# Taking the scores of a batch's new keys two steps earlier in a merged attention

## The chip, the core and the metric

The program runs on one core of a Trainium2 chip. The metric is the device time of one execution in microseconds (us). Before the change the median of three runs is 2041.23 us, from 2040.16 to 2042.34. All times of rows below come from one profiled execution of 2040.47 us, whose span from its first to its last instruction is 2038.8 us.

## What is computed

One inference step of a hybrid decoder layer, for a prompt of 1024 tokens and for 8 decoding batches of 8 new tokens each, every one with 4096 cached keys in 32 pages of 128. The part that matters here is differential attention: 4 heads, each with two query/key sub-heads of 64 dimensions and a value of 128. A decoding batch attends to its pages and, under a causal mask, to its own new keys, in one softmax:

```python
def diff_attend_sample(q, k, v, lam, k_past, v_past):
    s_past = jnp.einsum('bqhcd,bkhcd->bhcqk', q, k_past).astype(F32) * scale
    s_new = jnp.einsum('bqhcd,bkhcd->bhcqk', q, k).astype(F32) * scale
    s_new = jnp.where(jnp.tril(jnp.ones((T, T), dtype=bool)), s_new, -jnp.inf)
    a = jax.nn.softmax(jnp.concatenate([s_past, s_new], axis=-1), axis=-1)
    w = (a[:, :, 0] - lam * a[:, :, 1]).astype(v.dtype)
    return (jnp.einsum('bhqk,bkhv->bqhv', w[..., :P], v_past)
            + jnp.einsum('bhqk,bkhv->bqhv', w[..., P:], v))
```

The maximum of a softmax row thus spans the scores of all pages and those of the new keys. Projections, gated linear attention, output projection, feed-forward and a per-layer embedding stand before and after this part.

## The kernel before

The kernel is written in stages. The stage of interest, the function `attention`, merges two jobs in one order written out by hand: attention over the prompt (units of one head and 128 queries, 32 in all) and attention of the decoding batches over their pages. It lies between about 519 and 945 us of the span.

A group is 4 pages, 512 keys. A batch has NG = 8 groups, so there are NKV = 64. Every engine walks through the same steps t = 0 to 73, and in each it does what belongs to the step: the keys of group t are transposed (`turn_keys`, heads 0 to 3), scored against the batch's queries one step later (`score(t - 1)`), and their maximum and copy are taken by VectorE another step later (`max_scores(t - 2)`, `copy_scores(t - 2)`). The weights of group v = t - 9 (LAG = NG + 1) are made by ScalarE (`exps`), transposed (`turn_p`) and multiplied with the values (`values`): only when all 8 groups of a batch and its new keys are scored is its maximum known. Steps are counted by batch below: step 8b+9 is the end of batch b, where the last maximum is taken and the first weights are made.

Every second step has in between the prompt's work: `prompt_scores` on TensorE, which wait for ScalarE's last prompt exponentials; `prompt_maxima` on VectorE (mask, maximum, negated maximum), `prompt_exps` on ScalarE, `prompt_turn` (weights transposed) and `prompt_out` on TensorE.

What sets the order:
- The engines run their own lists in order; semaphores join them. An instruction that waits holds all that stands behind it on its engine.
- A ring of three PSUM banks (class `Ring`) takes every transposed key head, the transposed weights, the merge of a batch's output and the scores of the new keys, in the order in which TensorE fills them. A slot may be filled again when its last owner, three places before, has been emptied by ScalarE (key heads 0 to 2, merge) or by VectorE (the rest). `emptied(key)` is that wait on TensorE.
- The new keys of batch b: `score_new(b)` stands on TensorE at step 8(b+1), behind `score`. VectorE's `take_new(b)` stands in the next step between `max_scores` and `copy_scores`: it adds the mask into `dec_s` (which frees the ring slot, L1609), takes the maximum (L1611), the maximum over the nine columns of `mx` (L1613) and the negated scaled maximum (L1615), on which ScalarE's `exps` of the batch's first group wait.
- At a batch's end ScalarE makes the first weights (L1331), the weights of the new keys (L1336), and only then copies key head 2 (L1320, `take_keys(t, 2)`). The transpose of the new keys' weights (`turn_new_p`, L1454) has the ring slot that this copy empties.
- GpSimd asks for a group's value pages when the values of four groups before are done; SP for key pages when all heads of four groups before are transposed.

Names of rows: `dec_k`, `dec_v` pages; `dec_kt` transposed keys; `dec_s` scores; `dec_p`, `dec_pn` weights of a group and of the new keys; `att_p`, `att_wt` the prompt's weights and their transposes; `att_small` small columns such as maxima; `dec_osc` a batch's scaled output.

Of the kernel before, what the change touches and what calls it, by code (L numbers as in the profile page):

```python
# [15 lines left out]
ALU = mybir.AluOpType  # L16
ACT = mybir.ActivationFunctionType
AX = mybir.AxisListType
# [5 lines left out]
DB, DS = 8, 8  # L24
# [44 lines left out]
class Memory:  # L69


    def __init__(self, nc):
        self.nc, self.n = nc, 0
# [1021 lines left out]
NG = NPG // 4  # L1095
NKV = DB * NG
LAG = NG + 1
STEPS = NKV + LAG + 1
UNITS = [(h, i) for h in range(H) for i in (0, 7, 1, 6, 2, 5, 3, 4)]
NU = len(UNITS)  # L1100
# [7 lines left out]
def pieces_of(n):  # L1108
    return 1 if blocks_of(n) <= 4 else 2
# [6 lines left out]
class Ring:  # L1116
# [4 lines left out]
    def __init__(self):  # L1121
        self.index, self.emptied, self.owners = {}, {}, []
        count = {"act": 0, "dve": 0}

        def use(key, owner):
            self.index[key] = len(self.owners)
            count[owner] += 1
            self.emptied[key] = count[owner]
            self.owners.append((owner, count[owner]))

        for t in range(STEPS):
            if t < NKV:
                for h in range(H):
                    use(("keys", t, h), "act" if h < 3 else "dve")
            b, last = divmod(t - LAG - NG, NG)
            if last == 0 and 0 <= b < DB:
                use(("merge", b), "act")
            v = t - LAG
            if 0 <= v < NKV:
                if v % NG == 0:  # L1140
                    use(("new_p", v // NG), "dve")
                use(("p", v), "dve")
            b, last = divmod(t - NG, NG)
            if last == 0 and 0 <= b < DB:
                use(("new_s", b), "dve")

# [32 lines left out]
def attention(nc, io, m, ps, scr, sems):  # L1179
# [14 lines left out]
    d = {n: sems("p4_" + n) for n in names.split()}  # L1194
# [11 lines left out]
    W_BANK, S_BANK, O_BANK = bank(5), bank(6), bank(7)  # L1206
# [4 lines left out]
    mx, esum, ssum, cs, negm = (m.sc[:, 24:33], m.sc[:, 34:52].rearrange("p (u g) -> p u g", u=2), m.sc[:, 52:54],  # L1211
                                m.sc[:, 54:56], m.sc[:, 56:58])
# [18 lines left out]
    with nc.Block() as block:  # L1231
# [49 lines left out]
        def _(act):  # L1281
# [17 lines left out]
            def copy_weights(n, q):  # L1299

                i, u = UNITS[n][1], n % 2
                a, b = 4 * q * P, min(4 * q + 4, i + 1) * P
                act.wait_ge(s["turned"], pieces_before(n) + q + 1)
                if n >= 1:
                    act.wait_ge(s["o_done"], n)
                act.activation(m.wt[:, a:b], W_BANK[:, 0:b - a], ACT.Copy).then_inc(s["wt_copied"], 1)
# [33 lines left out]
            def copy_os(b):  # L1340
                act.wait_ge(d["ring_filled"], ring.filled(("merge", b)))
                act.activation(m.os[:, b, :], ring_bank(("merge", b))[0:32, 0:DV], ACT.Copy).then_inc(d["ring_act"], 1)

            for t in range(STEPS):
                v = t - LAG
                n, c = divmod(t, 2)
# [15 lines left out]
                if c == 1 and 0 <= n - 1 < NU and pieces_of(n - 1) == 2:  # L1362
                    copy_weights(n - 1, 1)
                if t >= LAG + NG and (t - LAG - NG) % NG == 0:
                    copy_os((t - LAG - NG) // NG)
                if t == HALVES:
# [8 lines left out]
        def _(pe):  # L1375
# [37 lines left out]
            def emptied(key):  # L1413
                before = ring.before(key)
                if before is not None:
                    pe.wait_ge(d["ring_act" if before[0] == "act" else "ring_dve"], before[1])
# [24 lines left out]
            def score_new(b):  # L1441
                if b == 0:
                    pe.wait_ge(d["new_in"], 32)
                key = ("new_s", b)
                emptied(key)
                for h in range(H):
                    ins = pe.matmul(ring_bank(key)[32 * h:32 * h + 32, 0:NS], m.qb[:, b % 2, h, :], m.kts[:, h, :],
                                    start=True, stop=True, tile_position=(0, 32 * h))
                ins.then_inc(d["ring_filled"], 1)
# [34 lines left out]
            def merge(b):  # L1484
                pe.wait_ge(d["final"], 4 * b + 4)
                emptied(("merge", b))
                pe.matmul(ring_bank(("merge", b))[0:32, 0:DV], const(m, "merge"), m.osc[:, :], start=True, stop=True
                          ).then_inc(d["ring_filled"], 1)

            pe.wait_ge(d["zero_done"], 4)  # L1490
            for t in range(STEPS):
                v = t - LAG
                n, c = divmod(t, 2)
                if t < NKV:
                    turn_keys(t, 0)
                    turn_keys(t, 1)
                if c == 0 and 0 <= n - 2 < NU:
                    prompt_out(n - 2)
                if c == 1 and 0 <= n - 1 < NU:
                    prompt_turn(n - 1, 0)  # L1500
                if t < NKV:
                    turn_keys(t, 2)
                    turn_keys(t, 3)
                if t >= LAG + NG and (t - LAG - NG) % NG == 0:
                    merge((t - LAG - NG) // NG)
                if 0 <= v < NKV:
                    if v % NG == 0:
                        turn_new_p(v // NG)
                    turn_p(v)
                if c == 1 and 0 <= n - 1 < NU and pieces_of(n - 1) == 2:  # L1510
                    prompt_turn(n - 1, 1)
                prompt_scores(t)
                if 1 <= t <= NKV:
                    score(t - 1)
                if t and t % NG == 0 and t // NG <= DB:
                    score_new(t // NG - 1)
                if 0 <= v < NKV:
                    values(v)

        @block.vector  # L1520
        def _(dve):
# [68 lines left out]
            def max_scores(k):  # L1590
                b, g = divmod(k, NG)
                dve.wait_ge(d["s_full"], k + 1)
                dve.tensor_reduce(mx[:, g:g + 1], S_BANK, AX.X, ALU.max)

            def copy_scores(k):
                b, g = divmod(k, NG)
                if b:
                    dve.wait_ge(d["exp_done"], k - NG + 1)
                dve.tensor_copy(m.ss[:, 512 * g:512 * g + 512], S_BANK).then_inc(d["s_taken"], 1)

            def take_new(b):

                key = ("new_s", b)
                dve.wait_ge(d["ring_filled"], ring.filled(key))
                dst = m.ss[:, PAST:PAST + NS]
                if b:
                    dve.wait_ge(d["expn_done"], b)
                a = CONST_COLS["past"][0] + 56 - b * DS
                dve.tensor_tensor(dst, ring_bank(key)[:, 0:NS], m.consts[:, a:a + NS], ALU.add).then_inc(d["ring_dve"], 1)  # L1609
                dve.wait_ge(d["ring_dve"], ring.emptied[key])  # L1610
                dve.tensor_reduce(mx[:, NG:NG + 1], dst, AX.X, ALU.max).then_inc(d["mx"], 1)  # L1611
                dve.wait_ge(d["mx"], b * 2 + 1)
                dve.tensor_reduce(ssum[:, 1:2], mx, AX.X, ALU.max).then_inc(d["mx"], 1)  # L1613
                dve.wait_ge(d["mx"], b * 2 + 2)
                dve.tensor_scalar(negm[:, b % 2:b % 2 + 1], ssum[:, 1:2], -SC, None, ALU.mult).then_inc(d["negm"], 1)  # L1615

            def take_new_p(b):
# [31 lines left out]
            queries(0)  # L1649
            for t in range(STEPS):  # L1650
                v = t - LAG
                n, c = divmod(t, 2)
                if t >= LAG + NG and (t - LAG - NG) % NG == 0:
                    finalize((t - LAG - NG) // NG)
                if 0 <= t - 2 < NKV:
                    max_scores(t - 2)
                if 0 < t - 1 <= NKV and (t - 1) % NG == 0:
                    take_new((t - 1) // NG - 1)
                if 0 <= t - 2 < NKV:
                    copy_scores(t - 2)  # L1660
                if t < NKV:
                    take_keys(t, 3)
                if 0 <= v < NKV:
                    if v % NG == 0:
                        take_new_p(v // NG)
                    take_p(v)
                if c == 0 and 0 <= n - 1 < NU:
                    prompt_combine(n - 1)
                prompt_maxima(t)
                if t % NG == 4 and t // NG + 1 < DB:  # L1670
                    queries(t // NG + 1)
                if t >= LAG + NG - 1 and (t - LAG - NG + 1) % NG == 0:
                    final_scale((t - LAG - NG + 1) // NG)
                if HALVES < t <= HALVES + H:
                    norm_prompt(t - HALVES - 1)
# [890 lines left out]
```

## Time and profile before

| what | value |
|---|---|
| median of three runs | 2041.23 us (2040.16 to 2042.34) |
| profiled execution, its own time | 2040.47 us |
| its span | 2038.8 us |
| TensorE busy, share of the span | 1863.9 us, 91% |
| TensorE weight loads | 1718.4 us, 84% |
| VectorE | 971.9 us, 48% |
| ScalarE | 608.9 us, 30% |
| GpSimd | 397.2 us, 19% |
| HBM traffic over the span | 114 GB/s |

Shares of the whole span are averages over stages with different limits. For a change within the merged attention only rows of that stage tell: who waits there, and for whom. A row of a timeline has the start in us, the time it took, engine, line, operation, what is written and read, a count, and in brackets how long the engine had been idle before it and what released it. PE is TensorE, PEld its weight loads, DVE is VectorE, ACT ScalarE, POOL GpSimd. Where TensorE works almost without a break, ends of matmuls overlap the next start, since they are pipelined.

### The profile page before, as it was taken

How to read it: one execution, taken by the hardware profiler on the slowest of the kernel's cores; microseconds unless marked ns; L12 is line 12 of the kernel's file. 1: busy time of each engine (PE TensorE's matmuls, PEld its weight loads, DVE VectorE, ACT ScalarE, POOL GpSimd, SP SyncE). 2: the span in 40 equal slices, each digit the busy share in tenths (PEclk: the TensorE clock that was granted, in tenths of full speed). 3: DMA queues.
4: the chain of work that ended last, by engine and by line, in shares of the span. 5: the costliest groups of instructions: out<-in, count | busy, mean ns of one | idle time of the engine just before them, and what ended most of it. 6: DMA issues, size and time to landing. Idle time of an engine off the chain costs nothing. (4 is left out here: it accounts for less than half of the span.)

```text
span 2038.8 us, 35290 instructions
## 1 busy us (share of the span) xinstructions
PE 1863.9 (91%) x13412; PEld 1718.4 (84%) x13412; DVE 971.9 (48%) x1356; ACT 608.9 (30%) x1086; POOL 397.2 (19%) x393
## 2 busy tenths in 40 slices
PE   4999999575899999996999999999999999998898
PEld 4999999463566767664898999999999999998798
DVE  4223730486677777775325334344334333436443
ACT  4113321442465655563322211111111111113320
POOL 1112420232123333332112011101101110104110
PEclk9999999696899999998999999999999999999899
DMA  4332640204799999987111111111111111110221
GB/s 141 97 85 76 156 114 21 65 3 145 247 329 348 360 337 366 356 257 228 32 42 52 47 47 32 52 43 49 45 42 42 42 53 42 32 54 20 85 64 44
DMA packets 201583, 239.02 MB, mean 117 GB/s; under 512 B 15425, under 2 KB 142354, under 8 KB 201426
## 3 DMA queue, kind: packets, MB, share of 16 engines
q1 hardware_dynamic: 180946, 169.75, 27.0%
q0 software_dynamic: 20480, 67.13, 9.7%
q8 instruction: 105, 1.72, 0.4%
q14 instruction: 52, 0.43, 0.1%
HBM read 215.44 MB, written 16.91 MB: 114 GB/s over the span
## 5 line engine op out<-in xcount | busy, mean ns | idle before, releaser
L150 PE MATMUL psum<-h_hi,w_hi 128*128 128x364 f32 x1248 | 278.7, 332 | 2.8 <-issue 2.8
L150 PE MATMUL psum<-h_lo,w_hi 128*128 128x364 f32 x1248 | 276.3, 330 | 0.0
L150 PE MATMUL psum<-h_hi,w_lo 128*128 128x364 f32 x1248 | 275.2, 328 | 0.0
L2078 ACT ACTIVATE w_hi<-w_raw 128x1024 fp32r<-128x1024 f32 x66 | 68.8, 1059 | 586.3 <-PE psum L150 565.5
L150 PEld LDWEIGHTS psum<-h_hi,w_hi 128*128 128x128 f32 x1248 | 215.4, 189 | 4.9 <-issue 4.2
L150 PEld LDWEIGHTS psum<-h_lo,w_hi 128*128 128x128 f32 x1248 | 217.1, 189 | 0.0
L150 PEld LDWEIGHTS psum<-h_hi,w_lo 128*128 128x128 f32 x1248 | 216.7, 188 | 0.0
L2054 POOL TENSOR_TENSOR w_raw<-w_raw,gains 128x1024 f32<-128x1024 f32 x42 | 80.5, 1916 | 652.2 <-DMA w_raw<-in_w_ffn_gate 353.0
L1163 POOL DMA_DIRECT2D dec_v<-in_cache_v x256 | 137.5, 537 | 316.6 <-issue 316.6
L150 PE MATMUL psum<-x_hi,w_hi 128*128 128x364 f32 x792 | 188.5, 347 | 9.7 <-DVE x_lo L1911 5.8
L150 PE MATMUL psum<-x_hi,w_lo 128*128 128x364 f32 x792 | 176.5, 331 | 0.0
L150 PE MATMUL psum<-x_lo,w_hi 128*128 128x364 f32 x792 | 176.3, 331 | 0.0
L2194 DVE TENSOR_TENSOR h<-h,psum 128x1092 f32<-128x1092 f32 x88 | 113.5, 1289 | 108.0 <-PE psum L150 108.0
L150 PEld LDWEIGHTS psum<-x_hi,w_hi 128*128 128x128 f32 x792 | 137.3, 191 | 16.5 <-DVE x_lo L1911 6.3
L1425 PE MATMUL psum<-consts,dec_k 128*128 128x128 f32 x1024 | 139.7, 281 | 12.2 <-DVE dec_s L1609 6.1
L1320 ACT ACTIVATE dec_kt<-psum 128x512 f32<-128x512 f32 x192 | 108.4, 599 | 139.8 <-PE psum L1425 139.8
L1425 PEld LDWEIGHTS psum<-consts,dec_k 128*128 128x128 f32 x1024 | 115.2, 143 | 31.6 <-issue 17.0
L150 PEld LDWEIGHTS psum<-x_lo,w_hi 128*128 128x128 f32 x792 | 139.4, 190 | 0.0
L150 PEld LDWEIGHTS psum<-x_hi,w_lo 128*128 128x128 f32 x792 | 138.9, 190 | 0.0
L2173 DVE TENSOR_TENSOR t_up<-psum,rstd_and_sum 128x1092 f32<-128x1092 f32 x22 | 28.5, 1296 | 205.9 <-PE psum L150 205.9
L150 PE MATMUL psum<-hidden_hi,w_hi 128*128 128x364 f32 x528 | 116.9, 330 | 2.5 <-DVE w_lo L2164 2.5
L150 PE MATMUL psum<-hidden_lo,w_hi 128*128 128x364 f32 x528 | 117.4, 331 | 0.0
(262 smaller groups left out, 2793.4 us busy)
## 6 DMA issues: line engine op xcount, KB each, us to landing
dec_k<-in_cache_k SPq DMA_DIRECT2D x256, 256.0 KB, 5.1
dec_v<-in_cache_v POOLq DMA_DIRECT2D x256, 256.0 KB, 5.2
w_raw<-in_w_in SPq DMA_DIRECT2D x25, 512.0 KB, 3.9
w_raw<-in_w_ffn_gate SPq DMA_DIRECT2D x22, 512.0 KB, 3.9
w_raw<-in_w_ffn_up SPq DMA_DIRECT2D x22, 512.0 KB, 3.8
w_raw<-in_w_ffn_down SPq DMA_DIRECT2D x22, 512.0 KB, 3.6
feat_swap<-feat_n SPq DMA_DIRECT2D x32, 136.5 KB, 2.4
x_in<-in_x_prompt SPq DMA_DIRECT2D x4, 1024.0 KB, 8.2
```

The costliest lines, as they stand in the source:

```text
L150: ins = pe.matmul(out[:, c, 0:SPAN], w(k), x(k)[:, c * SPAN:c * SPAN + SPAN], start=n == 0 and w is whi and x is xhi, stop=n == len(ks) - ...
L1163: eng.dma_start(ring[:, slot, p:p + 1, :], cache[bass.ds(page, 1)].rearrange("o t f -> t o f")).then_inc(sem, 16)
L1320: act.activation(m.kt[:, t % 2, h, :], ring_bank(("keys", t, h)), ACT.Copy).then_inc(d["ring_act"], 1)
L1425: ins = pe.transpose(ring_bank(key)[:, p * P:p * P + P], m.kr[:, t % KR, p, h * P:h * P + P], ident)
L2054: gp.tensor_tensor(m.raw[:, u], m.raw[:, u], gain(m, "ffn").unsqueeze(2).broadcast_to([P, KT, P]), ALU.mult).then_inc(s["w_scaled"], 1)
L2078: act.activation(m.whi[:, slot], m.raw[:, u], ACT.Copy).then_inc(s["w_hi"], 1)
L2173: dve.tensor_tensor(spans(dst), dense[bank][:, :, 0:SPAN], spans(m.rb[:, :]), ALU.mult).then_inc(s["evacuated"], 1)
L2194: dve.tensor_tensor(spans(m.h[:, n]), spans(m.h[:, n]), dense[n % 2][:, :, 0:SPAN], ALU.add).then_inc(s["evacuated"], 1)
```

## The change

`score_new` moves from step 8(b+1) to step 8b+6 of TensorE (NEW_AT = 6), and the entry of the ring with it. `take_new` keeps the mask add and the maximum of the new keys, and VectorE runs it in step 8b+7, behind the copy of that step's scores. The maximum over the nine columns and its scaling become `batch_max`, which stays at the batch's end. The last `max_scores` of a batch now raises the semaphore on which `batch_max` waits; before, the wait was on the new keys' maximum, which came behind it on the same engine.

```diff
+NEW_AT = NG - 2
...
-            b, last = divmod(t - NG, NG)
+            b, last = divmod(t - NEW_AT, NG)
             if last == 0 and 0 <= b < DB:
                 use(("new_s", b), "dve")
...
-                if t and t % NG == 0 and t // NG <= DB:
-                    score_new(t // NG - 1)
+                if t % NG == NEW_AT and t // NG < DB:
+                    score_new(t // NG)
                 if 0 <= v < NKV:
                     values(v)
...
-                dve.tensor_reduce(mx[:, g:g + 1], S_BANK, AX.X, ALU.max)
+                ins = dve.tensor_reduce(mx[:, g:g + 1], S_BANK, AX.X, ALU.max)
+                if g == NG - 1:
+                    ins.then_inc(d["mx"], 1)
...
                 dve.tensor_reduce(mx[:, NG:NG + 1], dst, AX.X, ALU.max).then_inc(d["mx"], 1)
-                dve.wait_ge(d["mx"], b * 2 + 1)
+
+            def batch_max(b):
+                dve.wait_ge(d["mx"], b * 3 + 2)
                 dve.tensor_reduce(ssum[:, 1:2], mx, AX.X, ALU.max).then_inc(d["mx"], 1)
-                dve.wait_ge(d["mx"], b * 2 + 2)
+                dve.wait_ge(d["mx"], b * 3 + 3)
...
                 if 0 < t - 1 <= NKV and (t - 1) % NG == 0:
-                    take_new((t - 1) // NG - 1)
+                    batch_max((t - 1) // NG - 1)
                 if 0 <= t - 2 < NKV:
                     copy_scores(t - 2)
+                if (t - 1) % NG == NEW_AT and (t - 1) // NG < DB:
+                    take_new((t - 1) // NG)
```

The orders of ScalarE, GpSimd and SP stay as they are. The changed file is a line longer at its head, so TensorE's lines count one more, VectorE's up to five.

TensorE, batch 1, from the prompt's scores of step 14 to the values of step 16, before (L1389 prompt scores, L1437 scores, L1447 scores of the new keys, L1479 values, L1425 key transposes, L1402 and L1460 transposes of the weights):

```order
L1389 MATMUL psum<-att_k_102,att_q 128x384 x2
L1437 MATMUL psum<-dec_kt,dec_qb 32x512 x4
L1479 MATMUL psum<-dec_v,dec_pt 32x128 x16
L1425 MATMUL psum<-consts,dec_k 128x128 x8
L1402 MATMUL psum<-consts,att_p 128x128 x4
L1425 MATMUL psum<-consts,dec_k 128x128 x8
...
L1389 MATMUL psum<-att_k_97,att_q 128x128 x2
L1437 MATMUL psum<-dec_kt,dec_qb 32x512 x4
L1447 MATMUL psum<-dec_new_k,dec_qb 32x64 x4
L1479 MATMUL psum<-dec_v,dec_pt 32x128 x16
```

The same stretch of TensorE in the changed kernel:

```order
L1390 MATMUL psum<-att_k_102,att_q 128x384 x2
L1438 MATMUL psum<-dec_kt,dec_qb 32x512 x4
L1448 MATMUL psum<-dec_new_k,dec_qb 32x64 x4
L1480 MATMUL psum<-dec_v,dec_pt 32x128 x16
L1426 MATMUL psum<-consts,dec_k 128x128 x8
L1403 MATMUL psum<-consts,att_p 128x128 x4
L1426 MATMUL psum<-consts,dec_k 128x128 x8
...
L1390 MATMUL psum<-att_k_97,att_q 128x128 x2
L1438 MATMUL psum<-dec_kt,dec_qb 32x512 x4
L1480 MATMUL psum<-dec_v,dec_pt 32x128 x16
```

The scores of the new keys stand in step 14, and the third key transpose behind them, in the ring's order, is head 2 of step 15.

VectorE, batch 1, steps 15 and 17 of the changed kernel; first step 15, from the maximum of the scores to the transposed weights (L1594 maximum, L1602 copy, L1612 mask add, L1614 maximum of the new keys, L1589 copy of key head 3, L1632 of the weights):

```order
L1594 TENSOR_REDUCE att_small<-psum 128x1
L1602 COPY dec_s<-psum 128x512
L1612 TENSOR_TENSOR dec_s<-psum,consts 128x64
L1614 TENSOR_REDUCE att_small<-dec_s 128x1
L1589 COPY dec_kt<-psum 128x512
L1632 COPY dec_pt<-psum 128x512
```

The third and fourth row are new in this step. At the batch's end, step 17, VectorE had before, from the scaled output to the copy of the scores:

```order
L1644 TENSOR_SCALAR dec_osc<-psum,att_small 128x128
L1593 TENSOR_REDUCE att_small<-psum 128x1
L1609 TENSOR_TENSOR dec_s<-psum,consts 128x64
L1611 TENSOR_REDUCE att_small<-dec_s 128x1
L1613 TENSOR_REDUCE att_small<-att_small 128x1
L1615 TENSOR_SCALAR att_small<-att_small 128x1
L1599 COPY dec_s<-psum 128x512
```

and has now:

```order
L1649 TENSOR_SCALAR dec_osc<-psum,att_small 128x128
L1594 TENSOR_REDUCE att_small<-psum 128x1
L1618 TENSOR_REDUCE att_small<-att_small 128x1
L1620 TENSOR_SCALAR att_small<-att_small 128x1
L1602 COPY dec_s<-psum 128x512
```

The mask add and the new keys' maximum are gone from this place.

## Rows read from the trace of the kernel before

**Rows 1.** Stretches: us, busy by engine (instructions), PEclk, DMA share, GB/s.

```profile
620.00:660.00 40.00, 38.14 (x481) 27.81 (x481) 28.99 (x57) 23.18 (x60) 13.41 (x25) 1.00 1.03 341
```

**Rows 2.** Waits for value pages and for the scores: engine, instruction, us, times.

```profile
  PE psum L1479: 8.7, 4
...
  DVE att_small L1615: 2.6, 7
...
  PE psum L1425: 6.1, 7
```

**Rows 3.** Timeline, all engines, end of batch 1 (step 17).

```profile
617.10 0.68 DVE L1593 TENSOR_REDUCE att_small<-psum 128x1 f32<-128x512 f32 x1
...
617.70 0.21 DVE L1609 TENSOR_TENSOR dec_s<-psum,consts 128x64 f32<-128x64 f32 x1
617.95 0.22 DVE L1611 TENSOR_REDUCE att_small<-dec_s 128x1 f32<-128x64 f32 x1
...
617.97 1.09 PE L1425 MATMUL psum<-consts,dec_k 128*128 128x128 f32 x8 [0.91 <-DVE dec_s L1609]
...
618.20 0.16 DVE L1613 TENSOR_REDUCE att_small<-att_small 128x1 f32<-128x9 f32 x1
618.40 0.15 DVE L1615 TENSOR_SCALAR att_small<-att_small 128x1 f32<-128x1 f32 x1
...
618.59 0.72 ACT L1331 ACTIVATE dec_p<-dec_s,att_small 128x512 f32<-128x512 f32 x1 [0.34 <-DVE att_small L1615]
...
618.99 0.41 PE L1487 MATMUL psum<-dec_osc,consts 128*32 128x128 f32 x2
...
620.36 0.30 PE L1454 MATMUL psum<-consts,dec_pn 128*128 128x128 f32 x1 [0.96 <-ACT dec_kt L1320]
```

**Rows 4.** Timeline, ScalarE, end of batch 2 (step 25).

```profile
668.81 0.72 ACT L1331 ACTIVATE dec_p<-dec_s,att_small 128x512 f32<-128x512 f32 x1 [0.21 <-DVE att_small L1615]
```

**Rows 5.** Timeline, TensorE, scores and values of steps 15 and 16.

```profile
608.03 1.07 PE L1437 MATMUL psum<-dec_kt,dec_qb 128*32 128x512 f32 x8
...
608.91 1.06 PE L1479 MATMUL psum<-dec_v,dec_pt 128*32 128x128 f32 x32
...
613.54 1.07 PE L1437 MATMUL psum<-dec_kt,dec_qb 128*32 128x512 f32 x8
...
614.54 1.06 PE L1479 MATMUL psum<-dec_v,dec_pt 128*32 128x128 f32 x32
```

**Rows 6.** Timeline, TensorE and VectorE, step 15 (8b+7 of batch 1).

```profile
605.35 1.04 PE L1425 MATMUL psum<-consts,dec_k 128*128 128x128 f32 x8
605.37 0.68 DVE L1599 COPY dec_s<-psum 128x512 f32<-128x512 f32 x1
...
606.22 0.60 PE L1460 MATMUL psum<-consts,dec_p 128*128 128x128 f32 x4
...
607.18 0.92 PE L1389 MATMUL psum<-att_k,att_q 64*128 64x384 f32 x4 [0.36 <-ACT att_p L1296]
...
608.14 0.43 DVE L1548 TENSOR_TENSOR psum<-psum,consts 128x256 f32<-128x256 f32 x1 [0.43 <-PE psum L1389]
```

**Rows 7.** Timeline, TensorE and VectorE, steps 7 (batch 0) and 23 (batch 2).

```profile
557.87 0.68 DVE L1599 COPY dec_s<-psum 128x512 f32<-128x512 f32 x1
...
559.17 1.13 PE L1389 MATMUL psum<-att_k,att_q 64*128 64x512 f32 x4 [1.01 <-ACT att_p L1296]
...
655.09 0.68 DVE L1599 COPY dec_s<-psum 128x512 f32<-128x512 f32 x1
...
657.11 1.13 PE L1389 MATMUL psum<-att_k,att_q 64*128 64x512 f32 x4 [0.58 <-ACT att_p L1296]
```

**Rows 8.** Timeline at the end of batch 7, then the stretch behind it.

```profile
917.38 0.48 PE L1454 MATMUL psum<-consts,dec_pn 128*128 128x128 f32 x1 [2.14 <-ACT dec_pn L1336]
...
922.28 0.54 POOL L1163 DMA_DIRECT2D dec_v<-in_cache_v  x1 [2.06 <-issue]
...
917.30:921.00 3.70, 3.62 (x47) 2.60 (x47) 0.98 (x2) 1.16 (x5) 1.61 (x3) 0.57 0.76 226
```

## The prediction

> **What bounds the kernel now.** I looked first at the stretch that the diff can touch, the merged attention between 519 and 945 us, by stretches. In a typical 40 us of it TensorE is busy for 38.14 us, VectorE for 28.99 and ScalarE for 23.18; the DMA engines are taken too, at 341 GB/s [rows 1]. Two bounds lie close together, so the waits have to decide. TensorE's waits for value pages are 8.7 us in 4 times [rows 2], all four after 930 us, where the last pages come in; for key pages it has none. Up to there the pattern of a batch repeats every 50 us (the same instruction starts at 618.59 and 668.81 [rows 3, 4]). So order and latency between engines bound this stage, not bytes, and time that TensorE gains or loses before its tail moves the end.
>
> Next I asked who waits for the new scores. TensorE's matmuls wait 6.1 us in 7 times for the mask add that frees their ring slot, and ScalarE 2.6 us in 7 times for the negated maximum [rows 2]. The first number looks like the prize. The timeline of one batch's end says otherwise.
>
> At the end of batch 1 (step 17) [rows 3], VectorE takes the last maximum at 617.10 us, then mask add, two reductions and the scaling at 618.40. The add ends at 617.91 and TensorE goes on at 617.97, after 0.91 us of waiting. But TensorE does not keep what it would win there: after two key transposes and the merge at 618.99 it stands again until 620.36, 0.96 us, for ScalarE, whose copy of key head 2 comes after both exponentials in its own order. ScalarE began the first at 618.59, having waited 0.34 us for the maximum. **Only those 0.34 us can be won.** Taking away the 0.91 us makes the second wait longer by as much. Batches 3 and 5 read the same; batches 2, 4 and 6 have 0.21 us in its place [rows 4], batch 0 nothing (7 waits for 8 batches), and batch 7 what is left of the 2.6: 2.6 - 3 x 0.34 - 3 x 0.21 = 0.95. **2.6 us is the ceiling.**
>
> **The change part by part.**
>
> *Batch end, VectorE.* Mask add and reduction leave, one wait comes in: the reduction over nine columns now waits for the last maximum to be written. That wait is not in the trace; the nearest one is that of the same reduction for the one before it: 617.95 plus 0.22, next start 618.20, so 0.03 us after the end [rows 3]. Its bounds are 0 and the 0.06 us that a release took to another engine; I take 0.03. The maximum lasts 0.68, so: 617.10 + 0.68 + 0.03 = 617.81 for the reduction, 0.20 later 618.01 for the scaling, where 618.40 was. **Gain 0.39 us** in the chain of the maximum. Behind the waiting reduction stand the copy of the last scores and the copy of key head 3, which come 0.39 earlier too.
>
> *Score matmuls, TensorE.* Four small matmuls move from step 8b+8 to 8b+6. With them a step's scores and values start 1.00 us apart (613.54 to 614.54), without them 0.88 (608.03 to 608.91) [rows 5]: 0.12 us that changes place. It issues no DMA, and the orders of ScalarE, GpSimd and SP are as before.
>
> *The new waiting place.* In a ring of three slots the third key transpose after the new scores gets their slot. That is now head 2 of step 8b+7 (b is the batch), and the mask add that frees it stands behind the copy of that step's scores. Batch 1, step 15 [rows 6]: copy at 605.37, add 0.60 later (the distance from maximum to add, 617.10 to 617.70), end after 0.21, TensorE 0.06 after that: 606.24. TensorE had begun these transposes at 605.35. So they come 0.89 us later, 0.77 of it waiting. Behind them stand head 3, the transposes of the weights, the prompt's scores, the batch's scores and the values. Weight transposes 0.87 later (605.35 to 606.22): 607.11; 0.60 for them: prompt scores at 607.71. They stood at 607.18, having waited 0.36 us for ScalarE, a chain that moves by the 0.12 only (607.30). That cover takes part of the wait, and **0.53 us** is left. The two added VectorE instructions there cost nothing more: the copy of head 3 behind them waits for TensorE anyway, and VectorE idled 0.43 us for the prompt scores at 608.14 [rows 6]. Those it waits for again, so from here all moves by 0.53: step 16's scores, its VectorE chain, and the last maximum of step 17.
>
> *Sum of a batch.* VectorE's maximum comes 0.53 - 0.39 = 0.14 us later. ScalarE was ready at 618.59 - 0.34 = 618.25 and is now at 618.25 + 0.53 - 0.12 = 618.66, before the 618.73 of the maximum. So the new weights, and with them TensorE, come **0.14 us later** in batches 1, 3 and 5, though the 0.91 us wait is gone. Batches 2, 4 and 6, step 23 for one [rows 7]: copy 655.09, add 655.69, TensorE 655.96, weights 656.83, prompt scores 657.43 where they stood at 657.11 (0.58 of cover): 0.32 later. Maximum 0.07 earlier; ScalarE, ready 0.21 earlier than it began, comes 0.20 later: it decides, 0.01 us earlier. Batch 0, step 7 [rows 7]: copy 557.87, TensorE 558.74; no weight transposes follow yet, so prompt scores 0.87 later at 559.61 for 559.17: 0.44, less 0.12, and ScalarE had not waited at the batch's end: 0.32 later. Batch 7, step 63, has the form of step 15: 0.14 later, and this reaches the end, since GpSimd starts the next page loads at 922.28 after 2.06 us of idling for a value step [rows 8].
>
> 0.32 + 3 x 0.14 - 3 x 0.01 + 0.14 = **0.85 us later**. The profiled execution would go from 2040.47 to 2041.3 us (span 2038.8 to 2039.7, with the 1.7 around it). It lies 0.76 below the median of the three runs; from the median 2041.23 I come to 2042.1.
>
> **Key and value pages.** SP's load of keys waits for head 3 of four steps before; that comes some 0.9 us later once in a batch. Four steps are 25 us of the batch's 50, and TensorE has waited for no key page, so I add nothing; if a page should be late after all, the price would be at most those 0.9 us less the cover, again within the range.
>
> **The rivals.**
> *The full gain.* If the add at step 8b+7 ran early enough not to hold TensorE, or its wait vanished in idle time, the ceiling stands: 2041.23 - 2.6 = 2038.6 us. For it: ScalarE's 2.6 us are real. Against: the copy and TensorE's transposes start within 0.02 us of each other (605.37, 605.35), and the slot comes after the copy.
> *The wait is not covered.* If the 0.89 us goes wholly into VectorE's chain, since the cover by ScalarE moves too, each batch loses 0.89 - 0.39 = 0.50: 8 x 0.50 = 4.0, and 2041.23 + 4.0 = 2045.2 us. The rows with 0.36 and 0.58 us of cover speak against it.
> *The clock, the slower side.* At batch 7's end TensorE waited 2.14 us in one piece, and the stretch after it, 917.3 to 921.0, shows a granted clock of 0.57, between the levels of 1.2 and 2.4 GHz [rows 8]; the new weights' transpose took 0.48 us there, 0.30 at batch 1 [rows 3, 8]. The change joins two waits into one: at batch 1 TensorE's key transposes would start at 617.97 - 0.91 + 0.41 = 617.47, the merge 1.02 later, through at 618.90, and TensorE would stand until 620.50: 1.6 us, where 0.91 and 0.96 stood apart. If that suffices for the drop, 3.7 us at 0.57 cost 0.43 x 3.7 = 1.6 us at each of seven ends: 11 us, and 2042.1 + 11 = 2053 us. It decides somewhere between 0.96 us, after which the clock stayed, and 2.14. Against it: TensorE's work around the batch's end is the same, only shifted.
> The Trainium skill (TensorE: Matmul & The Clock Gate, What's actually happening) says that the clock follows how busy the engine has lately been. By that rule the clock would stay, since the change hardly alters how much TensorE works and waits there, and the time would be the forecast's; the row after 2.14 us agrees in that the clock fell behind a pause.
> *It does not do what it says.* That the maximum is not nearer to the batch's end for ScalarE is my forecast already; its part in the time is priced above.
>
> **How the numbers follow.** Forecast (small shift, within some 1.5 us) 0.66; full gain 0.16; uncovered wait 0.12; clock 0.06. Some 0.2%, 4.1 us, is about what a measurement of this kernel can tell from no change. Forecast and full gain lie within it but for 0.02; the uncovered wait lies at its edge, half over; the clock is over. So faster 0.02, same 0.86, slower 0.12. The range goes from the full gain to the uncovered wait, 2038.6 to 2045.3 (with 0.1 for the median), and leaves out the clock and the outer ends.
>
> **What would show it.** In the changed profile TensorE should wait for the mask add 8 times some 0.8 us (1.5 in batch 0), now at step 8b+7; the wait of 0.91 us at the batch's end should be gone, and the one before the new weights' transpose should have grown from 0.96 to some 1.6 us. A batch should still take 50 us, within 0.2. A batch shorter by 0.3 us would show the full gain, by 0.5 longer the uncovered wait, and a granted clock under 1 at 620 us the clock.

## The result, and the profile after

The changed kernel takes 2045.91 us (median of seven runs, 2040.44 to 2050.30) where the kernel before takes 2040.44 in the runs beside it: ratio 1.0027, 95% interval 1.0014 to 1.0040. It is slower by some 5.5 us. The forecast was 2042.1, the range ended at 2045.3. Against the median of the runs beside it, the forecast shift of 0.85 us would have been 2041.3.

The profiled execution of the changed kernel is its fastest run, 2040.44 us with a span of 2038.8, the same as before. The loss is in its attention stage all the same: from the first key transpose to the first matmul of the output projection the stage takes 439.38 us (515.71 to 955.09), where it took 433.28 before (519.05 to 952.33). That is 6.1 us more. In this execution the part ahead of the stage, which is the same in both kernels, was 3.3 us shorter and the part behind it 2.8 us shorter.

First the step that I had costed. Timeline of step 15 of the changed kernel (start, us, engine, line, operation, count, in brackets the idle time before it), which answers to [rows 6]:

```profile
600.31 1.09 PE L1426 MATMUL psum<-consts,dec_k 128*128 128x128 f32 x8
...
601.59 0.68 DVE L1602 COPY dec_s<-psum 128x512 f32<-128x512 f32 x1
602.18 0.21 DVE L1612 TENSOR_TENSOR dec_s<-psum,consts 128x64 f32<-128x64 f32 x1
...
602.45 1.09 PE L1426 MATMUL psum<-consts,dec_k 128*128 128x128 f32 x8 [0.61 <-DVE dec_s L1612]
...
603.91 0.92 PE L1390 MATMUL psum<-att_k,att_q 64*128 64x384 f32 x4
```

The same step of the kernel before begins with

```profile
603.98 1.09 PE L1425 MATMUL psum<-consts,dec_k 128*128 128x128 f32 x8
```

The mask add comes 0.59 us after the copy, TensorE 0.06 after its end, and the prompt's scores no longer wait for ScalarE. From the first keys of the step (600.31) to these scores it is 3.60 us, where 603.98 to 607.18 were 3.20: 0.40 more, where the prediction has 0.53 less the 0.12 by which the step begins earlier. So this went as worked out, except that TensorE's wait is 0.61 us and not 0.77. Over the whole stage the waits for the scores' tile are (engine, instruction, us, times), answering to [rows 2]:

```profile
  DVE att_small L1620: 0.5, 1
...
  PE psum L1426: 4.5, 8
```

ScalarE's wait for the maximum is gone but for batch 7, and TensorE waits 8 times for the mask add at its new place: seven times 0.61 or 0.62 us, and in batch 0 only 0.20 (1.5 was expected), since it had already waited 1.07 us for a key page in the same step.

Then the batch's end. TensorE's merge and the transpose of the new keys' weights, with the scores behind them, at the ends of batches 1 and 2, answering to [rows 3]:

```profile
614.48 0.41 PE L1488 MATMUL psum<-dec_osc,consts 128*32 128x128 f32 x2
616.70 0.30 PE L1455 MATMUL psum<-consts,dec_pn 128*128 128x128 f32 x1 [1.81 <-ACT dec_kt L1321]
...
617.99 1.07 PE L1438 MATMUL psum<-dec_kt,dec_qb 128*32 128x512 f32 x8
...
666.93 0.30 PE L1455 MATMUL psum<-consts,dec_pn 128*128 128x128 f32 x1 [1.90 <-ACT dec_kt L1321]
...
669.20 1.93 PE L1438 MATMUL psum<-dec_kt,dec_qb 128*32 128x512 f32 x8
```

At the ends of batches 1 to 6 the two waits have become one of 1.81 to 1.91 us; at batch 0 it is 1.61, at batch 7 1.76. Behind batch 1 the eight score matmuls take 1.07 us as ever; behind batch 2 the same eight take 1.93. The view by stretches says why (start:end, length, busy us of PE, PEld, DVE, ACT, POOL, then the granted TensorE clock, DMA share, GB/s), for some 3.7 us behind the ends of batches 1 to 7 of the changed kernel:

```profile
616.70:620.40 3.70, 3.70 (x61) 2.55 (x62) 3.06 (x7) 1.13 (x4) 0.54 (x1) 1.00 1.02 322
...
666.90:670.60 3.70, 3.67 (x20) 1.77 (x24) 2.20 (x5) 1.34 (x4) 0.54 (x1) 0.62 1.06 354
...
718.50:722.30 3.80, 3.74 (x22) 1.90 (x26) 1.99 (x5) 1.13 (x4) 0.54 (x1) 0.56 1.03 343
...
770.20:774.00 3.80, 3.71 (x60) 2.46 (x60) 2.86 (x7) 1.34 (x4) 0.54 (x1) 1.00 1.05 384
...
820.30:824.00 3.70, 3.67 (x31) 1.95 (x35) 2.30 (x6) 1.13 (x4) 0.54 (x1) 0.65 1.05 345
...
872.00:876.00 4.00, 3.89 (x20) 2.08 (x24) 2.08 (x4) 1.34 (x4) 0.54 (x1) 0.57 1.05 346
...
920.31:924.11 3.80, 3.80 (x47) 2.74 (x47) 0.98 (x2) 1.13 (x4) 1.61 (x3) 0.55 0.82 247
```

and of the kernel before, behind the ends of batches 2, 3, 5 and 6:

```profile
670.58:674.38 3.80, 3.80 (x61) 2.50 (x62) 2.95 (x7) 1.34 (x4) 0.37 (x1) 1.00 1.05 360
720.49:724.29 3.80, 3.80 (x62) 2.65 (x63) 3.10 (x7) 1.13 (x4) 0.47 (x1) 1.00 1.05 343
...
820.69:824.49 3.80, 3.80 (x63) 2.71 (x64) 3.10 (x7) 1.13 (x4) 0.45 (x1) 1.00 1.04 340
870.91:874.71 3.80, 3.80 (x61) 2.50 (x62) 2.95 (x7) 1.34 (x4) 0.37 (x1) 1.00 1.03 347
```

In the changed kernel TensorE looks busy all the time, but behind four of these ends with a third to a half of the matmuls (20 to 31 in place of some 60). The granted clock fell to its lower level, 1.2 instead of 2.4 GHz, behind the ends of batches 2, 3, 5 and 6. In the kernel before it was 1.00 behind the ends of batches 0 to 6. Behind batch 7, the last, it fell in both kernels; below, ends are counted from batch 0 to 6, seven of them, unless batch 7 is named. The distances between successive transposes of the new keys' weights (us, batch 0 to 1, 1 to 2, and so on) show what a fall costs. The last column is the whole stage. The last two lines are of kernels of the next section in which no fall occurs behind any end, batch 7 included:

| kernel | 0-1 | 1-2 | 2-3 | 3-4 | 4-5 | 5-6 | 6-7 | stage |
|---|---|---|---|---|---|---|---|---|
| before | 50.37 | 50.22 | 49.91 | 50.30 | 49.90 | 50.22 | 46.47 | 433.28 |
| changed | 50.49 | 50.23 | 51.63 | 51.73 | 50.04 | 51.78 | 48.20 | 439.38 |
| changed, six extra matmuls (e1) | 50.50 | 50.17 | 50.05 | 50.16 | 50.05 | 50.17 | 46.61 | 435.39 |
| changed, two extra matmuls (e7) | 50.50 | 50.22 | 50.05 | 50.15 | 50.04 | 50.15 | 46.60 | 432.77 |

Against e7 the four batches with a fall are 1.58, 1.58, 1.63 and 1.60 us longer: 6.4 us together. The batches without one agree within 0.01. (One of e1's twelve runs took 6458.07 us; it counts in e1's median below, and its ratio leaves it out.)

### The profile page after: what moved, and what is told of

Read it like the earlier page. It is cut to its first block and busy times, and to the rows that moved or that the text cites. A ratio compares the mean times of both kernels' runs of the same rounds, so it can differ in the third digit from the quotient of the medians.

```text
span 2038.8 us, 35290 instructions
## 1 busy us (share of the span) xinstructions
PE 1864.1 (91%) x13412; PEld 1716.3 (84%) x13412; DVE 973.4 (48%) x1356; ACT 609.1 (30%) x1086; POOL 396.6 (19%) x393
```

## The experiments

Two theories stood at first: *clock* (the joined wait at a batch's end lets TensorE's clock fall) and *ring* (the new wait for the mask add at step 8b+7, or late key pages, cost the time). Each time below is the median of its runs, each ratio is to the kernel before in runs on the same chip, with its 95% interval; it is an estimate from all these runs, not the quotient of two medians. The falls are read from one profiled execution of each kernel.

**e1: work in the joined wait.** Edit on the changed kernel:

```diff
                     if v % NG == 0:
+                        for _ in range(6):
+                            pe.matmul(O_BANK[:, 0:DV], ident, ident, start=True, stop=True)
                         turn_new_p(v // NG)
```

> The changed kernel with six extra matmuls of the identity by itself at each batch's end, written to the output bank that is free there, ahead of the transpose of the new keys' weights. They take some 0.8 us out of the 1.8 us in which TensorE stands there. Theory clock (the joined wait lets TensorE's clock fall behind some batch ends, 1.5 us each): granted clock 1.0 behind every end of batches 0 to 6, time down by some 5 us to 2040 to 2042, ratio to before 1.000 to 1.001. Theory ring (the new wait for the mask add at step 8b+7, or late key pages, cost the time): nothing changes, 2046, ratio 1.0027.

2038.74 us, ratio 0.9994 (0.9985 to 1.0003). Behind the ends of batches 2, 3 and 5, in the view by stretches:

```profile
667.61:671.41 3.80, 3.80 (x61) 2.50 (x62) 2.96 (x7) 1.34 (x4) 0.54 (x1) 1.00 1.05 374
717.66:721.46 3.80, 3.80 (x63) 2.71 (x64) 3.10 (x7) 1.13 (x4) 0.54 (x1) 1.00 1.05 346
817.87:821.67 3.80, 3.80 (x63) 2.71 (x64) 3.10 (x7) 1.13 (x4) 0.54 (x1) 1.00 1.04 330
```

The six matmuls take more than planned: the wait is 0.28 to 0.38 us at the ends of batches 1 to 6, so they fill some 1.5 us of it. The clock stays at 1.00 behind every end, batch 7 too. The wait for the mask add is still there, 0.62 us at each step 8b+7. So *ring* falls: its wait is in place and the loss is gone. Late key pages do not explain it either: the changed kernel has one wait for a key page, 1.07 us in batch 0, ahead of any fall. The stage is 4.0 us shorter than the changed kernel's, where 6.4 were to be had; the distances of batches give 6.4 back, and part of it is lost again: 0.8 us up to the end of batch 0, where the wait for the mask add is 1.35 us here, and 1.6 us behind batch 7, where the granted clock of the last 36 us is 0.72 against 0.80 in the changed kernel.

**e2: the control.** The same six matmuls in the kernel before.

> Control: the kernel before with the same six matmuls at the same place, where TensorE stands for 0.96 us. Theory clock: no fall to prevent there, so 2040 to 2041, ratio 0.999 to 1.001. If filling alone makes a kernel faster whatever the wait, it would show here as some 5 us less.

2040.44 us, ratio 0.9998 (0.9989 to 1.0007). Filling alone does not make the kernel faster where the clock does not fall: its batches are 0.2 to 0.4 us longer, up to the end of batch 6, since the six matmuls take more than the 0.96 us of waiting. (Behind batch 7 there was a fall to prevent, and the clock is at 1.00 there in e2.)

**e3: TensorE's own work in the wait.** At a batch's end, step 8b+9, the transposes of the new keys' weights and of the first weights come behind the prompt's scores and the batch's last scores. Edit on the changed kernel:

```diff
-                if 0 <= v < NKV:
-                    if v % NG == 0:
-                        turn_new_p(v // NG)
-                    turn_p(v)
+                first = 0 <= v < NKV and v % NG == 0
+                if 0 <= v < NKV and not first:
+                    turn_p(v)
                 if c == 1 and 0 <= n - 1 < NU and pieces_of(n - 1) == 2:
                     prompt_turn(n - 1, 1)
                 prompt_scores(t)
                 if 1 <= t <= NKV:
                     score(t - 1)
+                if first:
+                    turn_new_p(v // NG)
+                    turn_p(v)
```

> The changed kernel with TensorE's own work put into the joined wait: at a batch's end the second transposes of the prompt's weights, the prompt's scores and the last scores of the step come ahead of the new keys' weights and the first weights. Some 1.6 us of matmuls fill the wait, and some 0.8 us come back behind it, where the values wait for VectorE's copies. Theory clock: no falls, 2046 less 5 less 8 x 0.8, so 2033 to 2037. Theory ring: only the 6 us of filling, 2038 to 2041.

2033.02 us, ratio 0.9963 (0.9951 to 0.9974). TensorE's timeline at the end of batch 1:

```profile
616.81 0.41 PE L1488 MATMUL psum<-dec_osc,consts 128*32 128x128 f32 x2
617.15 0.33 PE L1403 MATMUL psum<-consts,att_p 128*128 128x128 f32 x1
617.41 0.49 PE L1390 MATMUL psum<-att_k,att_q 64*128 64x128 f32 x4
617.98 1.06 PE L1438 MATMUL psum<-dec_kt,dec_qb 128*32 128x512 f32 x8
619.04 0.30 PE L1455 MATMUL psum<-consts,dec_pn 128*128 128x128 f32 x1
...
620.57 1.08 PE L1480 MATMUL psum<-dec_v,dec_pt 128*32 128x128 f32 x32 [0.43 <-DVE dec_pt L1634]
```

The 1.81 us are filled with scores, 0.43 come back in front of the values, and the clock is at 1.00 behind every end. A batch takes 48.9 and 49.5 us in turn.

**e4: the ring's wait taken away.** On the changed kernel, `take_new` in front of `copy_scores` at step 8b+7:

```diff
+                if (t - 1) % NG == NEW_AT and (t - 1) // NG < DB:
+                    take_new((t - 1) // NG)
                 if 0 <= t - 2 < NKV:
                     copy_scores(t - 2)
-                if (t - 1) % NG == NEW_AT and (t - 1) // NG < DB:
-                    take_new((t - 1) // NG)
```

> The changed kernel with the mask add and the maximum of the new keys ahead of the copy of step 8b+7's scores instead of behind it, which frees the ring slot 0.6 us earlier. Theory clock: the wait for the mask add goes from 0.6 to under 0.1 us, but the joined wait stays at some 1.8 us and so do the falls: 2042 to 2045. Theory ring: the loss goes with the wait, 2037 to 2040.

2044.05 us, ratio 1.0014 (1.0005 to 1.0022). TensorE now waits for the mask add only in batch 0 (0.74 us). Behind the ends of batches 1 to 4:

```profile
621.70:625.50 3.80, 3.80 (x26) 1.92 (x30) 2.01 (x6) 1.13 (x4) 0.54 (x1) 0.56 1.05 347
673.25:677.05 3.80, 3.80 (x20) 2.27 (x24) 1.70 (x4) 1.34 (x4) 0.54 (x1) 0.55 1.05 368
724.44:728.24 3.80, 3.80 (x26) 2.06 (x30) 2.00 (x5) 1.13 (x4) 0.54 (x1) 0.55 1.05 343
775.97:779.77 3.80, 3.80 (x61) 2.50 (x62) 2.96 (x7) 1.34 (x4) 0.54 (x1) 1.00 1.06 391
```

The ring's wait is gone, the falls are not: behind six of seven ends here, the first after a wait of 1.61 us at batch 0. The one batch without a fall, 4 to 5, takes 49.64 us, 0.40 less than in the changed kernel and 0.26 less than in the kernel before. That is what the ring's wait cost in this batch: without it and without a fall the move would have gained a little.

**e5: e3's order in the kernel before.**

> The kernel before with only TensorE's order at the batch's end changed as in e3: second transposes of the prompt's weights, prompt's scores and last scores ahead of the new keys' weights. TensorE still waits 0.9 us there for the mask add, and 0.96 us of waiting can be filled. Theory that the change of this case adds 0.1 us in a batch to odd batches and nothing to even ones once the clock is out of play: the same as e3 within 1 us, so 2032 to 2034. Theory that moving the new keys is worth something of its own when the wait is filled: 2 to 5 us above e3.

2035.74 us, ratio 0.9983 (0.9971 to 0.9996). TensorE still waits 0.91 or 1.00 us for the mask add at six ends. Neither e3 nor e5 has a fall behind any end. The stage is 429.89 us, 4.6 longer than e3's, and six of its seven distances between batches are 0.5 or 1.0 us longer. So with the wait filled, taking the new keys' scores earlier is worth something, as the second theory had it. The whole times alone would not settle it: their intervals overlap.

**e6: e3 and e4 together.**

> The changed kernel with both: the mask add ahead of the copy of the scores at step 8b+7 (e4) and TensorE's own work in the joined wait (e3). e4's batches without a fall were 0.4 us shorter than the changed kernel's. Theory clock: no falls, e3 less 8 x 0.4, so 2029 to 2031. If the two do not add up, since the wait for the mask add only made room: 2033.

2030.13 us, ratio 0.9949 (0.9930 to 0.9968), with a stage of 422.63 us. Batches take 48.48 and 49.34 us in turn: 0.4 and 0.2 less than e3's, and the clock is at 1.00 behind every end.

**e7 and e8: one wait or two.** Both have two of e1's matmuls instead of six; e8 holds them until the first weights are made:

```diff
                     if v % NG == 0:
+                        pe.wait_ge(d["exp_done"], v + 1)
+                        for _ in range(2):
+                            pe.matmul(O_BANK[:, 0:DV], ident, ident, start=True, stop=True)
                         turn_new_p(v // NG)
```

(e7 is without the wait.)

> The changed kernel with two extra matmuls (0.26 us) right at the start of the joined wait: one wait of some 1.5 us stays. Pair with e8, same work in the same stretch. If the length of the single wait decides: still some falls, 2041 to 2045. If the sum of waiting decides, e7 and e8 show equally many falls.

> The same two extra matmuls, held until the first weights of the batch are made, which is in the middle of the joined wait: two waits of some 0.7 to 0.9 us, as in the kernel before. If the length of the single wait decides: no falls, 2040 to 2041. If the sum of waiting decides: as many falls as e7.

e7 took 2034.38 us, ratio 0.9980 (0.9969 to 0.9990), e8 2035.10, ratio 0.9978 (0.9966 to 0.9990). The clock is at 1.00 behind every end of both. The ends of batch 1 in e7 and in e8:

```profile
617.23 0.30 PE L1455 MATMUL psum<-consts,dec_pn 128*128 128x128 f32 x1 [1.18 <-ACT dec_kt L1321]
...
618.23 0.71 PE L1511 MATMUL psum<-consts 128*128 128x128 f32 x4 [0.92 <-ACT dec_p L1332]
619.14 0.30 PE L1455 MATMUL psum<-consts,dec_pn 128*128 128x128 f32 x1 [0.19 <-ACT dec_kt L1321]
```

The two matmuls take 0.63 us out of the wait, not 0.26. TensorE's single wait in e7 is 1.18 or 1.26 us at batches 1 to 6, so a wait of 1.5 us, at which I had expected falls, was never tried; in e8 the waits are 0.92 and 0.19. With no fall in either, the pair does not tell the length of one wait from the sum of waiting. The times are lower than the stages (432.77 and 432.74 us) explain; e11 goes after that.

**e9: the converse.** The kernel before, with three small copies on ScalarE ahead of a batch's first weights:

```diff
                 if g == 0:
                     act.wait_ge(d["negm"], b + 1)
+                    for j in range(3):
+                        act.activation(m.junk[:, 42 * j:42 * j + 42], ident[:, 0:42], ACT.Copy)
```

> The converse: the kernel before, new keys where they were, with three small copies on ScalarE ahead of the first weights of each batch, some 0.8 us. They lengthen TensorE's second wait at the batch's end from 0.96 to some 1.8 us, with 0.9 us for the mask add before it as it was. Theory clock: besides 8 x 0.8 = 6 us for the copies, falls behind several ends at 1.5 us each, so 2049 to 2056. If what counts in the changed kernel is not the long single wait but the new place of the scores: no falls, 2046 to 2047.

2045.63 us, ratio 1.0023 (1.0013 to 1.0033). The copies took half of what I had planned. ScalarE and TensorE at the end of batch 1:

```profile
619.05 0.49 ACT L1327 ACTIVATE att_o_sq<-consts 128x42 f32<-128x42 f32 x3 [0.34 <-DVE att_small L1617]
...
621.20 0.30 PE L1456 MATMUL psum<-consts,dec_pn 128*128 128x128 f32 x1 [1.34 <-ACT dec_kt L1320]
```

The first weights start 0.40 us later (619.45 for 619.05), and the second wait is 1.34 us instead of 0.96, behind a first one of 0.92 as before. Behind the ends of batches 0, 5 and 6:

```profile
568.81:572.61 3.80, 3.55 (x20) 1.58 (x24) 2.19 (x5) 1.63 (x4) 0.00 (x0) 0.73 0.80 247
...
823.19:826.99 3.80, 3.80 (x26) 2.19 (x30) 1.99 (x5) 1.13 (x4) 0.07 (x1) 0.56 1.04 353
...
875.32:879.12 3.80, 3.80 (x61) 2.50 (x62) 2.96 (x7) 1.34 (x4) 0.00 (x1) 1.00 1.01 347
```

Falls behind two ends of seven, with the new keys where they always were. 8 x 0.40 + 2 x 1.6 = 6.4 us over 2039.31, the median of the kernel before in these runs, is 2045.7, close to the measured 2045.63; the ratio's interval allows a loss of 2.7 to 6.7 us.

**e10: one step instead of two.** `NEW_AT = NG - 1` in the changed kernel (with a guard for the first step).

> One size: the changed kernel with the new keys one step ahead (NEW_AT = NG - 1) instead of two. The ring wait moves to step 8b+8, the batch's end is the same. Theory clock: the joined wait of 1.8 us and the falls stay, 2043 to 2047. If the two steps were the cause: about 2040.

2044.38 us, ratio 1.0027 (1.0016 to 1.0038). TensorE waits 1.75 to 1.99 us at each end. Behind the ends of batches 0, 4 and 6:

```profile
566.89:570.69 3.80, 3.56 (x20) 1.59 (x24) 2.19 (x5) 1.62 (x4) 0.00 (x0) 0.72 0.81 243
773.12:776.92 3.80, 3.80 (x20) 2.16 (x24) 1.83 (x4) 1.34 (x4) 0.54 (x1) 0.55 1.04 386
875.95:879.75 3.80, 3.80 (x61) 2.47 (x61) 2.91 (x7) 1.34 (x4) 0.54 (x1) 1.00 1.02 344
```

Only the last of the seven is without a fall. TensorE waits for the mask add only in batch 0 (0.73 us), so here too the ring's wait is gone and the falls are not. One step or two makes no difference that these runs tell; the joined wait is in both.

**e11 and e12: why e7 and e8 were faster than their stage.** e11 is the kernel before with two matmuls at the batch's end, e12 is e6 with the same two.

> Control for e7 and e8, whose whole time lay 5 to 6 us under the kernel before although their attention stage is only 0.5 us shorter; in their feed-forward loops TensorE shows no issue gaps, 2.0 to 2.8 us of them in the others. The kernel before with the same two matmuls at the batch's end. If the number of instructions ahead of those loops decides the gaps: the same 3 us come off, 2034 to 2037, and no issue gaps. If the changed order of the new keys does: 2040, with the gaps.

> e6 (early mask add and TensorE's own work in the joined wait) with the two matmuls ahead of the new keys' weights. No falls as in e6. If the number of instructions decides the gaps of the feed-forward loops, they go here too: 2026 to 2029; otherwise as e6, 2030.

e11 took 2033.67 us, ratio 0.9965 (0.9951 to 0.9978), e12 2028.61, ratio 0.9940 (0.9927 to 0.9954). In the feed-forward part, which no edit touches, the groups of TensorE by line (line, engine, operation, count, busy us, mean ns, idle before and what ended it) between 1150 and 1880 us of the kernel before, e7 and e11 read:

```profile
L150 PE MATMUL psum<-h_hi,w_hi 128*128 128x364 f32 x922 | 202.8, 328 | 2.8 <-issue 2.8
...
L150 PE MATMUL psum<-h_hi,w_hi 128*128 128x364 f32 x914 | 200.7, 328 | 0.0
...
L150 PE MATMUL psum<-h_hi,w_hi 128*128 128x364 f32 x918 | 201.6, 328 | 0.0
```

e7, e8, e11 and e12, the four kernels with two matmuls added at each of eight ends, have no issue gaps there, and their feed-forward part takes 697.6 to 697.8 us. The ten others, with none or 48 matmuls added, have 1.7 to 2.8 us of gaps and take 699.4 to 701.3. So some 2 to 3.5 us of e7's and e8's advantage come from there, and it is not the new keys; e1, at 701.1 us, has none of it. Why the added instructions matter to these loops is not shown. e11 also has no fall behind batch 7, like e7 and e8. e12 and e6 are not told apart by their runs, whose intervals overlap: e12's batches are 0.4 to 0.5 us longer, since the two matmuls no longer fall into a wait, and its feed-forward part is 3.7 us shorter. By medians e12 beats the kernel before by 12 us and the changed one, which ran on another occasion, by 17.

## Why the prediction was wrong

**The ceiling held, and the sum is right in size.** The 0.91 us wait was not worth its size, as worked out, since ScalarE's chain decides when TensorE goes on: TensorE's wait for the mask add is gone from the batch's end, and no batch became shorter by anything near it. Without falls (e7 against before) the distances 0-1, 2-3, 4-5 and 6-7 are 0.13 or 0.14 us longer, where the sum had 0.14; 1-2 is equal, 3-4 and 5-6 are 0.15 and 0.07 shorter, where the sum had 0.01. Together that is 0.32 us longer, against 0.53. The 0.32 us for batch 0 are not shown: from the first key transpose to the end of batch 0 the kernel before takes 50.94 us, the changed one 50.50, e7 51.54, and e11, which has the new keys where they were, 51.36; key pages came late there in the changed kernel (1.07 us), e7 (0.67) and e11 (1.64). e7 and e11, with the same two matmuls and no fall behind any end, differ by 0.6 us in their stage (432.77 and 432.20), against 0.85 as predicted.

**The step that failed** is that the sum puts the clock at nothing, with a chance of 0.06 for its rival. The rival's mechanism was in the prediction, and its price was 1.6 us for a fall, at which the runs arrived as well (1.58 to 1.63). The small chance rested on the argument that TensorE's work around the batch's end is the same, only shifted. It is not enough that work and waiting are the same in sum: before, 0.91 us and 0.96 us stood apart with 1.4 us of transposes and the merge between, and the clock stayed; now 1.81 to 1.91 us stand in one piece, and it fell behind four of seven ends. The prediction had taken seven of seven or none, which is why its rival came to 2053; the profiles show four (changed kernel), six (e4) and six (e10). 0.85 + 4 x 1.6 is 7.2 us of loss in the stage; 6.1 were seen in the profile, where the stretch up to the end of batch 0 was 0.44 us shorter instead of 0.32 longer, and some 5.5 in the runs. The sign named for the clock, a value under 1 at 620 us, is the end of batch 1, where it stayed at 1.00.

**A near number by luck.** The rival of the uncovered wait came to 2045.2 us, 0.7 from the measured time. Its mechanism, 0.50 us more in each batch, is not what happened: the changed kernel's batches without a fall are 0.01 to 0.14 us longer than before, and those with a fall are 1.4 to 1.7 us longer.

**The page that I weighed** (the Trainium skill, TensorE: Matmul & The Clock Gate, What's actually happening) says that the clock follows how busy TensorE has lately been. The runs agree with that much: e1's and e7's extra matmuls in the wait keep the clock at 1.00. My conclusion from it, that the clock would stay, was wrong, and the rows at hand spoke for caution: 2.14 us of waiting at batch 7 had brought a fall, 0.96 none, and 1.6 lay between.

**The size of the wait** was off by 0.2 to 0.3 us: 1.6 predicted, 1.81 to 1.91 in the trace. At batch 1 the 0.21 comes apart: key transposes that nothing holds start 0.16 us before the matmuls ahead of them end (605.35 against 604.91 + 0.60), which the idle time of 0.91 does not count, and the merge follows them after 0.97 us, not 1.02. The same 0.16 makes the wait at the new place 0.61 instead of 0.77.

**Open.** What exactly of the waiting decides. Behind the ends of batches 0 to 6, by the longest single wait: up to 1.00 us no fall in seven (the kernel before), 1.16 to 1.26 none (e7), 1.34 to 1.36 two (e9), 1.61 to 1.91 four or six (changed kernel, e4), 1.75 to 1.99 six (e10). In this order the falls never become fewer. Ordered by the sum of waiting they do not line up: batches 1 to 6 of the kernel before have 1.87 or 1.96 us in two pieces and no fall, where 1.81 to 1.91 in one piece had four. But these are few ends, one execution of each kernel, and equal waits of one run end differently (1.89 us at batch 4 without, 1.82 at batch 3 with a fall). At batch 7, where other work stands around the wait, 1.73 us in e5 brought none and 1.76 in the changed kernel one.

## What to carry to other kernels

A wait that hides behind another one is worth nothing by itself, and taking it away may join two short waits of TensorE into one long enough for its clock to fall: cost the clock behind every wait that a change makes longer, also where the end of the wait stays where it is. Where a wait cannot be shortened, put work that has to be done anyway into it; here moving the prompt's and the batch's scores into the joined wait turned a loss of 5 us into a gain of 7 (e3), and with the earlier mask add of 10 (e6); the same move takes 4.5 us off the kernel before (e5). And look at the parts that a change does not touch before a few us are credited to it.

## What the runs showed of the hardware

Two matmuls more at each batch's end, 16 in all ahead of the feed-forward loops, took TensorE's issue gaps there to nothing (2.8 us in the kernel before, none in e11; 2.8 in e6, none in e12) and 3.5 to 3.7 us off a part of 701 us; 48 of them did not take the gaps away (2.5 us in e1, 2.1 in e2). In the view by stretches a TensorE whose granted clock has fallen shows as busy: 3.67 us of 3.70 with 20 matmuls at 0.62 behind batch 2 of the changed kernel, where 61 stood in 3.70 us at 1.00 behind batch 1.
